# Third tile's query rows loaded ahead of the half product's stores, copies and additions of weight sums issued one at a time, first chunk split ahead of the evictions

## What is computed

```python
n = rms_norm(h, norm1_g)
proj = n @ w_in
(q_att, c_kv, q_idx, k_idx, w_idx, r_q, r_k, r_v, r_gate, g_att, g_ret) = jnp.split(proj, points, axis=-1)
q = rms_norm(q_att.reshape(B, S, 8, 128), q_norm_g)
kv = rms_norm(c_kv, kv_norm_g) @ w_kv_up
k_sh, v_sh = jnp.split(kv, 2, axis=-1)
k_sh = rms_norm(k_sh, k_norm_g)
att = sparse_indexed_attention(q, k_sh, v_sh, q_idx, k_idx, w_idx, slopes)   # top 256 keys of a score, 8 heads
y_att = att.reshape(B, S, 1024) @ w_att_branch
ret = retention_chunkwise(r_q, r_k, r_v, gammas)                             # 4 heads, chunks of 128
ret = group_norm_heads(ret, ret_norm_g)
y_ret = (jax.nn.silu(r_gate) * ret.reshape(B, S, 1024)) @ w_ret_branch
mixed = jax.nn.sigmoid(g_att) * y_att + jax.nn.sigmoid(g_ret) * y_ret
h = h + mixed @ w_out
h = h + hierarchical_moe(rms_norm(h, norm2_g), ...)                          # top-1 group, top-2 experts of 16
```

## Time and profile before

| | us |
|---|---|
| median of three executions | 1481.03 (1477.44 to 1482.12) |
| the profiled execution, its own time | 1481.06 |
| its span | 1479.3 |
| PE busy | 1382.5 (93%) |
| DVE, ACT, POOL busy | 1115.9, 867.2, 752.1 |
| mean granted clock of PE, share of full speed | 0.965 |

### The profile page before, as it was taken

How to read it: one execution, slowest core, us unless ns; L and a number is a source line. 1 busy time by engine, 2 the same in 40 slices (tenths; PEclk the granted TensorE clock), 3 DMA queues, 4 the chain that set the end, 5 groups by cost and what they waited for, 6 DMA issues and landing times.

```text
span 1479.3 us, 19665 instructions
## 1 busy us (share of the span) xinstructions
PE 1382.5 (93%) x6518; PEld 1132.3 (77%) x6518; DVE 1115.9 (75%) x1549; ACT 867.2 (59%) x1524; POOL 752.1 (51%) x538
## 2 busy tenths in 40 slices
PE   6998999999999998699999999999996699999995
PEld 6887777878888887467767878887885588888884
DVE  6828999999999956565614457989554699999984
ACT  5237534435874786566633555363245388888884
POOL 4621467858686533221214645565341468665654
PEclk9997999999999998899999999999998699999998
DMA  5997689896857577889848877573436897989896
GB/s 192 362 254 136 163 238 356 202 279 195 283 185 239 198 237 254 202 216 248 192 146 288 206 213 249 192 249 104 166 116 235 319 286 183 327 235 348 263 274 77
DMA packets 153364, 336.75 MB, mean 228 GB/s; under 512 B 14896, under 2 KB 32688, under 8 KB 149040
## 3 DMA queue, kind: packets, MB, share of 16 engines
q1 hardware_dynamic: 112480, 228.54, 45.4%
q0 software_dynamic: 28496, 82.85, 26.3%
q10 hardware_dynamic: 12288, 24.12, 4.4%
HBM read 323.92 MB, written 125.83 MB: 304 GB/s over the span
## 4 chain that ended last, share of the span: by engine, by line
PE 53%; DMA 19%; DVE 9%; POOL 9%; issue 5%; ACT 3%; SPq 0%; DVEq 0%; ACTq 0%; POOLq 0%
PE ps L994 14%; PE ps L995 14%; PE ps L996 14%; DMA out<-e_y,dest 8%; DMA t_raw<-turned_dram 4%; PE ps L1315 4%; POOL w_lo L2664 4%; PE ps L1305 2%; DMA sums_dram<-in_w_in 2%; POOL n_lo L2751 2%; POOL out L2836 1%; DMA qrow<-proj_dram 1%; DMA sums_dram<-sums_dram 1%; DMA a_raw<-att_dram 1%; DVE dist L2131 1%
## 5 line engine op out<-in xcount | busy, mean ns | idle before, releaser
L2664 POOL TENSOR_TENSOR w_lo<-w_raw,w_hi 128x512 fp32r<-128x512 f32 (+1 forms) x264 | 377.3, 1453 | 337.9 <-ACT w_hi L1521 328.0
L1521 ACT CAST w_hi<-w_raw 128x512 fp32r<-128x512 f32 (+1 forms) x264 | 160.5, 617 | 285.8 <-PE ps L996 231.3
L994 PE MATMUL ps<-n_hi,w_hi 128*128 128x512 f32 x624 | 247.2, 396 | 13.8 <-POOL w_lo L2664 8.2
L995 PE MATMUL ps<-n_lo,w_hi 128*128 128x512 f32 x624 | 245.2, 393 | 0.0
L996 PE MATMUL ps<-n_hi,w_lo 128*128 128x512 f32 x624 | 245.0, 393 | 0.0
L2602 DVE TENSOR_TENSOR e_lo<-e_raw,e_hi 128x2048 fp32r<-128x2048 f32 x93 | 213.2, 2295 | 22.4 <-ACT e_hi L1964 22.2
L994 PE MATMUL ps<-w_hi,n_hi 128*128 128x512 f32 (+1 forms) x528 | 202.7, 384 | 7.5 <-POOL w_lo L2664 7.5
L995 PE MATMUL ps<-w_lo,n_hi 128*128 128x512 f32 (+1 forms) x528 | 201.2, 381 | 0.0
L996 PE MATMUL ps<-w_hi,n_lo 128*128 128x512 f32 (+1 forms) x528 | 201.2, 381 | 0.0
L1964 ACT CAST e_hi<-e_raw 128x2048 fp32r<-128x2048 f32 x93 | 177.7, 1915 | 32.2 <-PE ps L996 16.2
L2836 POOL DMA_INDIRECT out<-e_y,dest x62 | 147.8, 2385 | 95.7 <-DMA out<-e_y,dest 68.2
(11 more groups left out here) (288 smaller groups left out, 2689.7 us busy)
## 6 DMA issues: line engine op xcount, KB each, us to landing
w_raw<-sums_dram SPq DMA_DIRECT2D x128, 256.0 KB, 3.9
e_raw<-in_w_gate SPq DMA_DIRECT2D x64, 512.0 KB
e_raw<-in_w_up SPq DMA_DIRECT2D x64, 512.0 KB
e_raw<-in_w_down SPq DMA_DIRECT2D x32, 1024.0 KB
w_raw<-in_w_in SPq DMA_DIRECT2D x80, 256.0 KB, 4.4
sums_dram<-in_w_in POOLq DMA_DIRECT2D x20, 1024.0 KB, 10.3
sums_dram<-in_w_in SPq DMA_DIRECT2D x16, 1024.0 KB, 10.7
sums_dram<-sums_dram POOLq DMA_DIRECT2D x16, 1024.0 KB, 8.6
```

The lines of the kernel that those rows point to most:

```text
L994: mm(out, a[0], b[0], start=first, stop=False, skip_group_check=skip)
L995: mm(out, a[0], b[1], start=False, stop=False, skip_group_check=skip)
L1521: nc.scalar.copy(w_hi[c % NH][:, :width], split_from(c)[:, :width]).then_inc(hi_ready, 1)
L2664: G.tensor_tensor(w_lo[c % NH][:, :width], split_from(c)[:, :width], w_hi[c % NH][:, :width].bitcast(F32), ALU.subtract).then_inc(lo_ready, 1)
```

## The change

It edits five places.

1. The start: ACT casts chunk 0 before the evictions, POOL subtracts it after the fifth tile's scale, and DVE squares the last tile after its first four evictions.
2. Block `qi`: POOL subtracts two chunks ahead of its wait for the row sums.
3. `add_sums` can issue the first addition of stage 0 alone. For groups 2 and 3 the second one, to m7, is issued four chunks later. The four copies of group 7 are issued one each behind four chunks of m7.
4. Retention: head 1's state scan stands ahead of what is left of the picks, of which the last four instructions now follow the first kept half; tile 0's queries are cast before ACT's Exp on one column (which loads its table) and subtracted by DVE ahead of head 3's scaling.
5. Attention's start: SP loads the third tile's rows ahead of `store_first(3)`. POOL scales them ahead of group 4's copies, and each addition of group 4 moves one tile later; group 5's copies keep their tile but stand behind the last sum of group 4.

```diff
--- before.py
+++ after.py
@@ -855,8 +855,8 @@
                 bk.wait_read(sp, ("rT", 2, j, half))
                 row = (2 * 2 + j) * P
                 sp.dma_start(ret_dram[row:row + P, half * BANK:(half + 1) * BANK], rT_out[n][:]).then_inc(ret_stored[n % 2], 16)
+            load_q(2)
             store_first(3)
-            load_q(2)
             def load_sum(i, at):
                 sp.dma_start(f_sum[at][:], t_dram[i * BANK:(i + 1) * BANK, :].rearrange("(k p) s -> p k s", p=P)).then_inc(gate_in, 16)
             sp.wait_ge(dist_done, NT)
@@ -1536,9 +1536,8 @@
                       scale=gains[:, G1 + k:G1 + k + 1]).then_inc(nhi_done, 1)
             square_x(SQ_ACT)
             act.wait_ge(const_in, 16 * 2)
-            turned_hi(0, range(0, 4))
             hi(0)
-            turned_hi(0, range(4, KT))
+            turned_hi(0)
             for c in range(1, NH):
                 hi(c)
             turned_hi(1)
@@ -1766,9 +1765,9 @@
                     hi(c + 1)
                     hi(c + 2)
                     hi(c + 3)
-            A(small[:, 497:498], small[:, 500:501], ACT.Exp)
             out_qT(0, 0)
             out_qT(0, 1)
+            A(small[:, 497:498], small[:, 500:501], ACT.Exp)
             out_turn(3)
 
             for m in range(STEPS + LAG + 4):
@@ -2043,9 +2042,9 @@
                                        op0=ALU.mult, op1=ALU.add, accum_out=small[:, t:t + 1]).then_inc(sq_dve, 1)
             for t in range(5):
                 norm_x(t)
-            square_x(NT - 1)
             dve.wait_ge(const_in, 16 * 2)
             turned_lo(0, range(0, 4))
+            square_x(NT - 1)
             for t in range(5, NT):
                 norm_x(t)
             turned_lo(0, range(4, KT))
@@ -2154,6 +2153,9 @@
                     dve.wait_ge(o_sq, NT * h + c + 1)
                     inst = V.scalar_tensor_tensor(ro[h % 2][:, c, :], ro[h % 2][:, c, :], small[:, 104 + c:105 + c], gate[:, c, :], ALU.add, ALU.mult)
                 inst.then_inc(o_gated, 1)
+                if h == 3:
+                    for g in range(2):
+                        out_qT(0, g)
                 dve.wait_ge(o_gated, h + 1)
                 dve.wait_ge(o_rstd, h + 1)
                 for c in range(NT):
@@ -2268,9 +2270,8 @@
                 if c == 105:
                     out_phase1(0)
                 pick(1.43)
-            pick(8)
             out_phase1(1)
-            pick(3)
+            pick(4)
             out_phase2(0)
             keep_first(0)
             pick(3)
@@ -2290,8 +2291,6 @@
                 pick(1e9)
             out_turn(2)
             out_phase2(3)
-            out_qT(0, 0)
-            out_qT(0, 1)
             keep_first(3)
             for m in range(STEPS + 1):
                 if m < STEPS:
@@ -2673,13 +2672,17 @@
                 else:
                     pool.wait_ge(sq_dve, 1)
                 rstd(small[:, 8 + t:9 + t], small[:, t:t + 1], 1, D, (rstd1, 1))
-            for c in range(NH - 1):
+                if t == 4:
+                    lo(0)
+            for c in range(1, NH - 1):
                 lo(c)
             ahead("kv")
+            for k in range(2):
+                lo(number["qi"] * KT + k + NH - 1)
             pool.wait_ge(kv_sq, 1)
             rstd(small[:, 32:40], small[:, 16:24], NT, KVL)
             rstd(small[:, 40:48], small[:, 24:32], NT, DI, (kv_rstd, 1))
-            def add_sums(stage, groups):
+            def add_sums(stage, groups, parts=2):
 
                 done = 64 * groups[0] if groups[0] < 4 else 128 * groups[0] - 192
                 if stage == 0:
@@ -2687,8 +2690,8 @@
                         pool.wait_ge(sums_in, 64 * (groups[0] + 1))
                     pool.wait_ge(sums_added, done)
                     for g in groups:
-                        G.dma_start(sum_rows(g, "m5"), quarter(g, 1, 1), accum_op=ALU.add).then_inc(sums_added, 16)
-                        G.dma_start(sum_rows(g, "m7"), quarter(g, 1, 0), accum_op=ALU.add).then_inc(sums_added, 16)
+                        for name, r, q in (("m5", 1, 1), ("m7", 1, 0))[:parts]:
+                            G.dma_start(sum_rows(g, name), quarter(g, r, q), accum_op=ALU.add).then_inc(sums_added, 16)
                 if stage == 1:
                     pool.wait_ge(sums_added, done + 32 * len(groups))
                     for g in groups:
@@ -2698,12 +2701,14 @@
                     for g in groups:
                         G.dma_start(sum_rows(g, "m3"), sum_rows(g, "m6"), accum_op=ALU.add, max_dma_last_dim=8192).then_inc(sums_added, 16)
 
-            def copy_sums(groups):
+            COPIES = (("m7", 0, 0), ("m5", 1, 0), ("m6", 0, 0), ("m3", 0, 1))
+
+            def copy_sums(groups, parts=COPIES):
                 pool.wait_ge(sums_added, 128 * groups[0] - 256)
                 for g in groups:
-                    for name, r, q in (("m7", 0, 0), ("m5", 1, 0), ("m6", 0, 0), ("m3", 0, 1)):
+                    for name, r, q in parts:
                         G.dma_start(sum_rows(g, name), quarter(g, r, q)).then_inc(sums_added, 16)
-            for k in range(KT):
+            for k in range(2, KT):
                 lo(number["qi"] * KT + k + NH - 1)
                 if k in (4, 7):
                     add_sums(k // 5, (0,))
@@ -2755,7 +2760,10 @@
                 for x in pieces_at(c):
                     turned_n_lo(x)
                 if c in adds_at:
-                    add_sums(*adds_at[c])
+                    add_sums(*adds_at[c], parts=1)
+                if c - 4 in adds_at and adds_at[c - 4][0] == 0:
+                    g, = adds_at[c - 4][1]
+                    G.dma_start(sum_rows(g, "m7"), quarter(g, 1, 0), accum_op=ALU.add).then_inc(sums_added, 16)
             pool.wait_ge(q_squares, 1)
             scale_q(0, NT)
             for i in range(4):
@@ -2768,12 +2776,13 @@
                 if i == 2:
                     scale_rows(0)
             scale_rows(1)
+            scale_rows(2)
             copy_sums((4,))
-            for t in range(2, NT):
+            for t in range(3, NT):
                 scale_rows(t)
-                if t < 5:
-                    add_sums(t - 2, (4,))
-                elif t == 5:
+                if t < 6:
+                    add_sums(t - 3, (4,))
+                if t == 5:
                     copy_sums((5,))
                 elif t == 6:
                     add_sums(0, (5,))
@@ -2794,11 +2803,11 @@
             for b in blocks[m6 // KT:number["wo1b"]]:
                 for k in range(KT):
                     lo(number[b[0]] * KT + k + NH - 1)
-                    if k == 2 and b[0] in REST[1:]:
+                    if b[0] == REST[1] and k < 4:
+                        copy_sums((7,), COPIES[k:k + 1])
+                    if k == 2 and b[0] in REST[2:]:
                         stage = REST.index(b[0]) - 1
-                        if stage == 0:
-                            copy_sums((7,))
-                        else:
+                        if stage:
                             add_sums(stage - 1, (7,))
             for k in range(KT):
                 lo(number["wo1b"] * KT + k + NH - 1)
```

## The result

Three runs of the changed kernel took 1462.07 us at the median (1461.47 to 1464.09), against 1481.03 before; the ratio is 0.9881, with a 95% interval of 0.9851 to 0.9911. The forecast was 1464.5, range 1457.5 to 1474.0. The profiled execution took 1461.47, its span is 1459.7.

What follows compares the result with a forecast made beforehand. PE, busy 93% of the span, was taken as the bound, through its idle stretches and low-clock matmuls. The terms 0 - 1.0 - 3.5 + 0.3 - 1.2 + 0.7 - 7.6 - 4.2 = -16.5 gave 1464.5 us, range 1457.5 to 1474.

Steps and rivals of the forecast that it cites:

- The third tile's rows: Attention's start: loading them ahead of four stores removes PE's 7.58 us wait wholly; -7.6 us, other end -4.
- the last copies: Last group's copies, one per chunk: PE's 2.99 us idle and slow matmuls behind it go; -4.2 us, end -2.
- The state scan: Head 1's state scan no longer stands behind the last pick, so PE's 1.21 us at 504.98 goes; -1.2.
- The turned queries and the port: Tile 0: 1.23 us idle at 577.45 goes; POOL holds VectorE up to 1.9 more; +0.7, ends -1.2 and +1.9.
- The first chunk: Start: the 4.67 us stall moves to chunk 1, low clock possible behind; 0, ends -0.4 and +1.6.
- Two w_lo early: Splits ahead of keys' statistics: PE's 2.09 us at 68.9 goes, part returns at keys' scale; -1.0, ends -2.1 and 0.
- Group 2: Additions issued one at a time: the load lands before PE needs it near 186.5; -3.5, ends -5.4 and 0.
- Group 3: No PE idle stretch at its additions, later addition meets fuller queues; +0.3, ends 0 and +2.
- A: Rival: transfers are the bound, later loads eat PE's lead at 70 and 186; 1469.7 us; chance 0.18.
- B: Rival: the fourth tile's rows come late instead, giving back 0.7 to 2.7 us; about 1468; chance 0.12.
- C: Rival, slower: POOL's chain of sums becomes the bound; a loss of 4.4 us needs it 36 us late; chance 0.03.
- the slack of m6's splits: POOL's w_lo for m6 against PE's first need at 760.92: some 15 us, so later sums cost nothing.

Runs made afterwards that it cites:

- the repair: The change with stages 1 and 2 of group 2's sums three chunks later (11 and 17 in place of 8 and 14): 1463.69 us, ratio 0.9898.
- the copies first: The change with POOL issuing group 4's four copies ahead of scaling the second and third tile's rows: 1462.99 us, ratio 0.9904.

## Why the prediction was right

- **The third tile's rows** (-7.6) and **the last copies** (-4.2) carried it. Both came in every profile that had them, -7.8 to -8.7 and -4.9, and went when they were undone. Reading the load's 17.35 us against an empty stretch of the DMA share was enough for the first.
- **The state scan** (-1.2) gave -1.5. **The turned queries and the port** (+0.7) gave +1.0, and the scaling was 5.83, in the 5 to 6 that I named. The mechanism stood; holding POOL for 2.4 us takes it away.
- **The first chunk** (0, at most +1.6) cost 2.2 (means of 3.0 with the part and 0.8 without). The step that failed is "20.5, ready at 21.4" for the second chunk's split, which began at 22.13. Three sizes were wrong in it. I let the cast start at once, but it waits 0.83 us for the chunk's load, and `n_lo` began at 16.55. I gave the square 0.6 us behind `n_lo`, where it takes 1.22. And I gave POOL's scale of the last tile 0.9 us, where its two instructions took 1.62 (20.51 to 22.13), twice the 0.82 of the tile before (17.79 to 18.61), while VectorE was scaling rows; that the port did this is likely and was not tried. The low clock behind two idle stretches, my upper bound, was also there. So the sign that I had named came: PE idle for as long as before, with slow matmuls behind.
- **Two w_lo early** (-1.0) gave -2.4. The step "their landing follows the queues' load" was wrong: ACT's wait at the keys' scale is 1.94 us before and after, 124.84 and 125.35, and 1.93 or 1.94 in all fourteen profiles. POOL's two operations for that scale set it, not the additions, so what was won at 70 us stayed won.
- **Group 2** (-3.5) gave nothing. I had worked out POOL's wait at 4 to 5 us, and it was 4.42; the step that failed is that it lies "against some 8 that POOL is ahead". PE waited 3.21 of the 4.42, a wait of several us at chunk 12, which I had named as a sign of being wrong. And the repair showed a second limit behind it, VectorE's additions of half products.
- **Group 3** (+0.3, nothing to win) won 2 to 3. The additions have no idle stretch beside them, but those at 306 and 330 us came back in both later profiles with the additions together, and I had looked only beside the issue.
- **Rivals.** A, that the transfers would eat the lead, was wrong for the lead at 70 us and right in its result for group 2, by another cause. B did not come: wherever the third tile's rows went ahead, the only wait of PE for scaled query rows over 0.3 us is one of 1.07 us, at 620.35 in the change. C did not come. (In the slack of m6's splits "53 less 8" should read 23 less 8, from 737.95 to 760.92; the 15 us are right.)
- **Behind the edits** the change won 4.5 us that I had not forecast. Every kernel run later won 1.3 to 3.1 us between 1030 and the end, the one with the third tile's rows alone and the one without them too. No part of the change is in all of them, so the profile of before was probably slow there by chance. Another 1.6 came at 1023: the same wait of 1.85 us is followed by low clock in before and five of the others, and not in eight.

The forecast came 2.4 us above the median. With the terms as measured by the means of the table, the parts of the change are worth about 2.2 - 2.4 - 0.8 - 3.1 - 1.5 + 1.0 - 7.9 - 4.6 = -17 us. That this lies so near the forecast's -16.5 is luck in the smaller terms, of which four were off by 1.4 to 3.4 us, and no luck in the two large ones.

## What to carry to other kernels

An engine that waits is not always in the way, and one that does not wait can be: taking away POOL's pause at a sum moved PE's wait to VectorE, whose addition came no sooner (218.67 against 218.54). Before filling an idle stretch of one engine of a pair that shares a port, ask what the other does there; a wait of 2.4 us on the engine with slack was worth 2.3 us of PE's time at the place. And look for a transfer's price behind its issue too, not only beside it: the waits that came back with group 3's additions stood 38 and 63 us behind them.

## What the runs showed of the hardware

- VectorE's instructions on six numbers per partition, 0.17 us at their shortest, took 4.46, 6.27 and 8.38 us beside POOL's runs, and ended with the run and not with POOL's first instruction. The kernel before has one of 9.22 us (170.02 to 179.24, POOL's run to 179.20), the change one of 7.32. In its scaling of `ro`, one instruction stood for each of POOL's two scalings in the change (2.02 and 1.98 us), and a single one through two issues and both scalings with the copies first (5.12). Why it gets a turn in the one case and not in the other was not tried.
- POOL's issuing of DMAs can hold VectorE: an instruction of 0.35 us that began at 571.02 was not done when the issues ended at 572.20.
- The granted clock behind an idle stretch of 1.85 us of PE, at the same matmul of the same products, fell to between 0.50 and 0.56 over 2 us in six of the fourteen profiles and stayed at 1.00 in eight.
